# Two buffers in turn for the single adaptive-norm tiles of a two-block transformer on one core

## The reference, cut to what matters

```python
for l in range(DEPTH):
    mod  = silu(c)     @ w_ada[l] + b_ada[l]     # 1024 -> 9 * 1024
    modc = silu(c_ctx) @ w_ada[l] + b_ada[l]
    sh1, sc1, gt1, sh2, sc2, gt2, sh3, sc3, gt3 = split(mod, 9)
    h = h + 0.5 * gt1 * swiglu(rms_norm(h, g) * (1 + sc1) + sh1, w1, w3, w2)
    ...
```

## Time and profile before

| what | us |
| --- | --- |
| median of three runs | 3005.26 |
| span of the profiled execution, first to last instruction | 3003.9 |
| TensorE busy in it | 2897.1 (96%) |
| VectorE busy | 2051.9 (68%) |
| ScalarE busy | 1366.5 (45%) |
| GpSimd busy | 153.3 (5%) |
| mean granted TensorE clock | 0.987 of full |

### The profile page before, as it was taken

How to read it: one execution, slowest core, us unless ns; L and a number is a source line. 1 busy time by engine, 2 the same in 40 slices (tenths; PEclk the granted TensorE clock), 3 DMA queues, 4 the chain that set the end, 5 groups by cost and what they waited for, 6 DMA issues and landing times.

```text
span 3003.9 us, 59994 instructions
## 1 busy us (share of the span) xinstructions
PE 2897.1 (96%) x23648; PEld 2789.5 (93%) x23648; DVE 2051.9 (68%) x3323; ACT 1366.5 (45%) x2212; POOL 153.3 (5%) x222
## 2 busy tenths in 40 slices
PE   8999999999999999999999999999999999899998
PEld 8889999888999999998889999999999999779998
DVE  4658786658678777778764476867768566876655
ACT  5555445555446432354544354223542235545543
POOL 0000000000000000010000020000200001000000
PEclk9999999999999999999999999999999999999999
DMA  6435764435666565552212354544645445225454
GB/s 235 146 115 187 243 235 163 149 108 176 211 210 198 193 222 194 177 184 67 81 45 89 105 185 161 206 156 171 208 162 207 144 152 187 64 82 192 161 184 138
DMA packets 148053, 487.54 MB, mean 162 GB/s; under 512 B 16400, under 2 KB 25872, under 8 KB 147728
## 3 DMA queue, kind: packets, MB, share of 16 engines
q1 hardware_dynamic: 126688, 407.22, 41.0%
q0 software_dynamic: 21168, 77.60, 7.6%
HBM read 482.66 MB, written 1.05 MB: 161 GB/s over the span
## 4 chain that ended last, share of the span: by engine, by line
PE 82%; DVE 9%; ACT 4%; issue 3%; DMA 2%; POOL 0%; DVEq 0%; ACTq 0%; SPq 0%; POOLq 0%
PE bank L2042 23%; PE bank L2043 22%; PE bank L2044 22%; DVE wlo L1141 3%; ACT whi L606 2%; PE bank L1960 2%; PE bank L1961 2%; PE bank L1962 2%; DVE acc L1742 2%; PE aux L2269 1%; PE bank L2287 1%; DMA bbb<-in_w_ada 1%; PE bank L2120 1%; DMA raw<-in_w_stream 1%; DMA big<-in_w_ada 1%
## 5 line engine op out<-in xcount | busy, mean ns | idle before, releaser
L2042 PE MATMUL bank<-uhi,whi 128*128 128x256 f32 x4968 | 1397.0, 281 | 9.6 <-DVE wlo L1141 6.0
L2044 PE MATMUL bank<-uhi,wlo 128*128 128x256 f32 x4968 | 1381.1, 278 | 0.0
L2043 PE MATMUL bank<-ulo,whi 128*128 128x256 f32 x4968 | 1380.9, 278 | 0.0
L1141 DVE TENSOR_TENSOR wlo<-raw,whi 128x1024 fp32r<-128x1024 f32 (+4 forms) x850 | 951.0, 1121 | 370.7 <-ACT whi L606 362.2
L2042 PEld LDWEIGHTS bank<-uhi,whi 128*128 128x128 f32 x4968 | 935.1, 188 | 28.2 <-issue 22.9
L606 ACT CAST whi<-raw 128x1024 fp32r<-128x1024 f32 (+4 forms) x850 | 811.5, 961 | 282.7 <-PE bank L2044 179.3
L2043 PEld LDWEIGHTS bank<-ulo,whi 128*128 128x128 f32 x4968 | 934.8, 188 | 3.4 <-issue 3.0
L2044 PEld LDWEIGHTS bank<-uhi,wlo 128*128 128x128 f32 x4968 | 937.7, 189 | 0.0
L2042 PE MATMUL bank<-yhi,whi 128*128 128x256 f32 x1740 | 494.1, 284 | 16.2 <-DVE wlo L1141 8.5
L2043 PE MATMUL bank<-ylo,whi 128*128 128x256 f32 x1764 | 491.3, 279 | 0.0
L2044 PE MATMUL bank<-yhi,wlo 128*128 128x256 f32 x1740 | 484.5, 278 | 0.0
(11 more groups left out here) (297 smaller groups left out, 2939.0 us busy)
## 6 DMA issues: line engine op xcount, KB each, us to landing
raw<-in_w_stream SPq DMA_DIRECT2D x674, 512.0 KB, 3.7
big<-in_w_ada POOLq DMA_DIRECT2D x64, 512.0 KB, 3.6
vt<-in_w_ada POOLq DMA_DIRECT2D x51, 512.0 KB, 3.7
raw<-in_w_stream SPq DMA_DIRECT2D x80, 256.0 KB, 2.7
raw<-in_w_stream SPq DMA_DIRECT2D x48, 384.0 KB, 3.1
bbb<-in_w_ada POOLq DMA_DIRECT2D x29, 512.0 KB, 4.7
raw<-in_w_stream SPq DMA_DIRECT2D x32, 192.0 KB, 2.4
raw<-in_w_stream SPq DMA_DIRECT2D x16, 128.0 KB, 2.0
```

The source lines that it names most:

```text
L1141: ve.tensor_tensor(wlo[:, u % SLOTS, 0:n], raw[:, u % SLOTS, 0:n], whi[:, u % SLOTS, 0:n].bitcast(F32), ALU.subtract).then_inc(s_low, 1)
L2042: te.matmul(out_, whi[:, u % SLOTS, w], hi(k)[:, cols], start=k == 0, stop=False)
L2043: te.matmul(out_, whi[:, u % SLOTS, w], lo(k)[:, cols], start=False, stop=False)
L2044: ins = te.matmul(out_, wlo[:, u % SLOTS, w], hi(k)[:, cols], start=False, stop=k == plan.kt[u] - 1)
```

## The change

In a stage with one tile per turn, tile `i` goes to buffer `i % 2`. The first two tiles of the stage are issued together at its head, and the load of tile `i` waits for the sums of tile `i - 2`. VectorE takes the buffer and the landing count by `i % 2` and `i // 2`; since these are numbers of the written program and not of a loop register, the stage's loop on VectorE and GpSimd is written out (the empty `then`). Stages with two or more tiles per turn are as before.

```diff
+ALTERNATE = 2
...
-            for s in range(n):
-                loads[s] += iters
+            for s in range(ALTERNATE if n == 1 else n):
+                loads[s] += (iters + ALTERNATE - 1 - s) // ALTERNATE if n == 1 else iters
...
+                def load_single(i):
+                    n, r = P * D, i % ALTERNATE
+                    to = ring(name)[r]
+                    pool.dma_start(to, w_ada[(first + i) * n:(first + i + 1) * n].rearrange(
+                        "(p a b) -> p a b", p=P, a=to.shape[1])).then_inc(s_ada_land[r], 16)
...
-                for r in range(per):
-                    load(r, None)
+                for r in range(ALTERNATE if per == 1 else per):
+                    if per == 1:
+                        load_single(r)
+                    else:
+                        load(r, None)
...
-                if plan.count[name] > SLOTS:
+                if per == 1:
+                    for i in range(ALTERNATE, plan.count[name] // SLOTS):
+                        pool.wait_ge(s_ada_sum, 2 * (first + i + 1 - ALTERNATE))
+                        load_single(i)
+                elif plan.count[name] > SLOTS:
...
-                    if s == 0:
+                    if per == 1:
+                        r = i % ALTERNATE
+                    if s == 0 and per == 1:
+                        dve.wait_ge(s_ada_land[r], 16 * (loads[r] + i // ALTERNATE + 1))
+                    elif s == 0:
                         dve.wait_ge(s_ada_land[r], 16 * i + 16 * (loads[r] + 1))
...
+                if plan.ada.get(name, (0, 0))[1] == 1 and then is None:
+                    then = lambda j: None
```

## The result

| | before | after |
| --- | --- | --- |
| median of five runs beside each other | 3005.29 (3005.05 to 3022.96) | 2985.27 (2978.53 to 2990.21) |
| profiled execution, its own time | not shown | 2987.72 |
| its span | 3003.9 | 2985.9 |

The ratio is 0.9919 with a 95% interval of 0.9892 to 0.9946: faster, by 20.0 us (0.7%) in the medians. Later runs of the same two kernels put the difference of the means at 14.5 us (3004.8 and 2990.3) and 17.1 us (3003.8 and 2986.7). Two executions of the kernel before, of 4044.16 and 5963.75 us, stand far outside all others and are counted in no mean or range here. What is to be explained is thus some 15 us that the change gives, and 3 to 5 us by which the medians of five differ more than the later means do.

The account below looks back on a forecast made before the run. TensorE, busy 2897.1 of 3003.9 us, bounds the kernel and stops when VectorE's sums wait for tile loads. Terms -4.56 - 1.41 - 1.1 + 0.5 - 4.2 = -10.8, plus 0.3, give -10.5: 2994.8 us, range 2988.5 to 3000.5.

Parts of the forecast that it names:

- The circle: up10: load and sums make a 13.70 us turn against TensorE's 11.3; loading a turn ahead breaks it, -4.56 us there.
- Rival 1: up10, down10, fdown100: VectorE stays late by its own work, leaving about a third of gains (3.4 us): 2998.2; chance 0.13.
- The early tile: Stage heads: issuing the first two tiles together competes with weight loads; +0.3 us in all, bounds 0 and +9.4.
- Rival 2: out0 and out1: the early tile slows the weight loads, half the dear bound, +4.7 us: 2999.5; chance 0.08.
- the row at 323.30: down00: two tiles issued together beside the weight stream with TensorE always busy, read as showing the early tile costs 0.
- Cadence, the size of the unknown: 256-column matmuls start every 117.8 or 113.4 ns, either possible after a hold-up; about 2 us each way.
- the falls: Clock falls in later idle places: 2 us added to the uncertainty, each worth up to 1.5 us.
- rival 4: After fdown100: some 100 quick units turn to the slow cadence, costing 10.9 us, touched stages 1.5: 3007.2; chance 0.04.
- VectorE's waits there go, TensorE's time stays: 0: up00 and up11: TensorE already hides VectorE's waits for tiles, so removing them gains 0 us.
- +0.3 stays: fdown100: unit 3's subtraction still stands behind a residual update and a sum, so +0.3 us remains; net -4.2.
- The loops unrolled ... 0: Touched stages: register arithmetic and branches go, but VectorE is ahead or waits, so 0 us; bounds -1 and +1.
- Rival 3: Touched stages at 113.3 ns per matmul and up11 too, -4.7 and -1.8 us: 2988.5; chance 0.12.

Follow-up runs that it names:

- thin sums: Changed kernel with the sums of the one-tile-per-turn stages cut to an eighth of their columns: 2983.2 us mean over 6 runs, ratio 0.9928.
- loops written out: Kernel before with only its loops written out, still one buffer, each load after the previous tile's sums: 2996.1 us mean over 12 runs, ratio 0.9972.
- half a turn of lead: Changed kernel, but each load issued after the first sum of the tile before, one tile at the head: 2993.7 us mean over 12 runs, ratio 0.9955.
- forced stops: Changed kernel with TensorE made to wait at every fourth unit of fup210 to fup212 for a subtraction two units further: span 3021.0 us, single execution.

## Why the prediction was wrong

In the main its mechanism was right:

- **The circle.** The waits inside the stages are gone, `up10` takes 36.88 (forecast 36.7) with no fall of the clock, `down10` the forecast 22.61. That the sums, short of the wait, still stand ahead of a subtraction costs nothing: the timeline shows VectorE catching up at 8.6 us per turn, and the thin sums change nothing in `up10`. Rival 1 was wrong.
- **The early tile.** Priced at 0.3 us. `out0` and `out1` are 0.05 longer and 0.21 shorter, `merge0` 0.45 longer. Rival 2 and its 4.7 us were wrong; the row at 323.30 was the right one to read.
- **down11** went to the slow cadence, +0.83: inside what was allowed for.

What failed, the larger first:

1. **"Cadence, the size of the unknown"**: "about 2 us each way", plus 2 for the falls. Cadence is drawn again along the whole span, not in the touched stages only. Over the profiles of this study it is worth from 19.0 us (4255 slow matmuls, the kernel after) to 44.1 (9863), and single executions of the kernel before lie between 2988.3 and 3023.4. The prediction took the step from "then may come out either way" to rival 4, found "some 100" units there that could turn, and then gave it a chance of 0.04, partly because "three runs agree within 0.24 us". The two runs of the same kernel that came next beside the result gave 3018.23 and 3022.96. Why the first three agreed is open: by the later scatter it is rare (of all triples of the 79 later times of the kernel before, about one in 5000 lies within 0.24 us). Nor does the cadence only turn where TensorE is "held up": it turned behind short matmuls with no stop as well. One kernel's executions have a standard deviation of 8.5 us (35 runs of the kernel before) and 6 to 8 (the kernel after), so even a forecast of -10.5 would have needed a range that reaches below 2988. In the first two profiles the tail gained 7.4 by cadence and other places gave 5.1 back.
2. **The stages, each read from one execution, and against the slow cadence.** The terms took each window's excess over 117.8 ns per matmul, though parts of these windows ran at 113.3. At equal cadence the first two profiles differ by 14.8 us in the ten stages, where the sum had 10.8: `up10` with `down10` by 7.1 (it had 6.0), `up12` with `down12` by 2.1 (1.1), `fup100` with `fdown100` by 5.6 (3.7). In that execution `up00` happened to escape, hence "VectorE's waits there go, TensorE's time stays: 0". Where the loads stop TensorE differs each time. Set out at equal cadence, in us, two stages each (`up11` and `down11` 66.2 both times in the first pair):

| | before, three profiles | loops written out | after, three profiles |
| --- | --- | --- | --- |
| `up00`, `down00` | 75.4, 81.4, 80.5 | 74.9 | 75.4, 75.2, 75.1 |
| `up10`, `down10` | 82.0, 78.2, 76.5 | 76.1 | 74.9, 74.9, 74.9 |
| `up12`, `down12` | 51.2, 51.5, 51.3 | 52.1 | 49.1, 50.5, 50.5 |
| `fup100`, `fdown100` | 72.2, 72.4, 71.7 | 71.3 | 66.6, 66.6, 67.4 |

   The means give -3.9, -4.0, -1.3 and -5.2, in all -14.4. The prediction had 0, -6.0, -1.1 and -3.7. Against these means `up10` was too dear, for it was read from the worst of the three; `up00` was missed altogether. In `fdown100` the "+0.3 stays" did not stay (21.83 us, where 22.4 to 23.2 were forecast), and `fup100` gained, where it was to lose 0.5, since its window of 39.11 hid stops behind the quick cadence.
3. **"The loops unrolled ... 0"** was right for the change as a whole, since half a turn of lead covers these 0.6 us per turn; but the reason given ("VectorE is ahead or waits") was wrong for the kernel before. There VectorE's wait was part of the circle, and the work behind it counted: written-out loops alone bring 7.1, in one profile.

So the change gives 14.4 us of the 20.0 by which the medians of five differ. The rest, 5.6 us, is no larger than the scatter of such a difference (about 6 us, one standard deviation, by drawing fives from the runs of both kernels), and nothing else was found for it. Rival 3 came nearest to the measured time, but not for its reason: in the first profile after, `up10` and `down10` ran at the slow cadence. (Its sum also gives 2988.3, not 2988.5.)

The Trainium skill (TensorE: Matmul & The Clock Gate, "Wait — 56ns, not 53.3ns?") has a single warm start-to-start time, 109.2 ns as an estimate for 256 columns. No profile of this study shows it: there are 113.3 and 117.8, and which of them is what the prediction needed to know.

## What to carry to other kernels

When a buffer's load waits for its last reader and that reader's successor waits for the load, add up the whole circle (reads, issue, landing, wake-up, work between) and set it against the turn of the engine that bounds the kernel: waits inside a shorter circle are free, and in a longer one each 0.1 us is paid every turn. Here half a turn of lead ended it. Read such a term from several executions of the kernel, with the matmul's cadence taken out, since one profile shows only where the stops fell that time. And measure how far one kernel's own executions lie apart before stating a range: three equal times are no measure of it.

## What the runs showed of the hardware

- **Two cadences of the same matmul at full clock**, 113.3 and 117.8 ns from start to start (records of 276 and 281 ns), unchanged over hundreds of matmuls, and turned at some of the places where TensorE is held up (3 of 12 forced stops) or where short matmuls of another shape stand with no stop (1 of 60 extra ones). Between the profiles here they are worth 19.0 to 44.1 us of 3000. Executions of one kernel lay up to 35 us apart; that cadence makes most of this was seen in the profiled ones only. What decides at a turn is open.
- **A wait in a loop, with register arithmetic beside it, costs more than the same wait written out on a constant**: 0.7 against 0.3 us from the end of the sum to the issue on GpSimd, 0.25 against 0.02 from the landing to VectorE's start. The loop, the register in the wait and the one in the load's address were not taken apart. Whether loads with an address from a loop register also land later (6.33 against 5.42 us) is open; it was not tried by itself.
- **A 512 KB load beside the weight stream** landed after 4.2 to 8.2 us inside the circle, so a circle that just fits in one execution does not in the next.
- None of the variants is clearly better than the changed kernel: at equal cadence the spans of half a turn (2954.1) and of the changed kernel (2956.6 to 2960.9) differ by about as much as two profiles of the same kernel.
